# A two-layer Hyena and neighbourhood-attention step on one Trainium2 core: filter stage and input projection rewritten

## What is computed

```python
def hyena_filters(L, pe_w1, pe_b1, pe_w2, pe_b2, pe_w3, sin_freq, decay):
    ...
    hdn = jnp.sin(sin_freq[0] * (feats @ pe_w1 + pe_b1))
    hdn = jnp.sin(sin_freq[1] * (hdn @ pe_w2 + pe_b2))
    k = (hdn @ pe_w3).astype(jnp.float32) * (jnp.exp(-t * jnp.abs(decay)) + MOD_SHIFT)
    return k[:, :D_MODEL], k[:, D_MODEL:]          # k_fwd, k_bwd

def hyena_mixer(u, w_in, sconv_w, sconv_b, k_fwd, k_bwd, bias, w_out):
    z = centred_conv3(u @ w_in, sconv_w, sconv_b)
    x0, x1, v = jnp.split(z, 3, axis=-1)
    y = bidir_long_conv(v * x1, k_fwd, k_bwd, bias) * x0
    return y @ w_out
```

## Time and profile before

| | |
|---|---|
| median of 3 runs | 3693.0 us (3691.22 to 3696.77) |
| profiled execution | 3697.59 us, its span 3695.8 us |
| TensorE matmul busy | 3504.7 us, 95% of the span |
| VectorE / ScalarE / GpSimd busy | 1540.4 / 1036.7 / 1241.4 us |
| mean granted TensorE clock | 0.977 |

### The profile page before, as it was taken

The page is one execution under the profiler, slowest core; times in us unless marked ns, Lnnn a source line. Parts: engine busy times, 40 slices in busy tenths (PEclk is TensorE's granted clock), DMA queues, the critical chain, the costliest instruction groups (busy, mean ns, idle before and its releaser), DMA issues. The chain is left out here.

```text
span 3695.8 us, 47103 instructions
## 1 busy us (share of the span) xinstructions
PE 3504.7 (95%) x19104; PEld 3039.2 (82%) x19104; DVE 1540.4 (42%) x2528; ACT 1036.7 (28%) x1558; POOL 1241.4 (34%) x819
## 2 busy tenths in 40 slices
PE   7899998989999999999989998999989999999997
PEld 6888887778788888888878878888878888888886
DVE  7855544565344434444431015777340222111116
ACT  4421211233511111111342215777343111111113
POOL 5421114534422222222451304666352222222223
PEclk9899999999999999999999999999999999999998
DMA  3443325662122221221253446776201111111111
GB/s 133 129 170 109 108 81 175 215 229 74 52 75 74 77 72 63 69 69 63 80 180 126 163 164 171 177 177 155 92 23 41 40 40 35 40 40 35 41 41 63
DMA packets 173814, 365.92 MB, mean 99 GB/s; under 512 B 16967, under 2 KB 98439, under 8 KB 171944
## 3 DMA queue, kind: packets, MB, share of 16 engines
q1 hardware_dynamic: 168168, 352.55, 30.1%
q10 hardware_dynamic: 5440, 10.49, 0.9%
HBM read 285.38 MB, written 77.59 MB: 98 GB/s over the span
## 5 line engine op out<-in xcount | busy, mean ns | idle before, releaser
L150 POOL TENSOR_TENSOR w_lo<-w_raw,w_hi 128x1024 fp32r<-128x1024 f32 x207 | 502.8, 2429 | 1451.9 <-ACT w_hi L144 1451.8
L158 PE MATMUL ps_r<-a_hi,w_hi 128*128 128x512 f32 (+1 forms) x2496 | 889.8, 356 | 18.5 <-POOL a_lo L1933 10.6
L158 PE MATMUL ps_r<-a_lo,w_hi 128*128 128x512 f32 (+1 forms) x2496 | 885.7, 355 | 0.0
L158 PE MATMUL ps_r<-a_hi,w_lo 128*128 128x512 f32 (+1 forms) x2496 | 884.3, 354 | 0.0
L158 PEld LDWEIGHTS ps_r<-a_hi,w_hi 128*128 128x128 f32 x2496 | 473.5, 190 | 95.8 <-POOL a_lo L1933 18.6
L158 PEld LDWEIGHTS ps_r<-a_lo,w_hi 128*128 128x128 f32 x2496 | 473.7, 190 | 65.4 <-issue 1.2
L158 PEld LDWEIGHTS ps_r<-a_hi,w_lo 128*128 128x128 f32 x2496 | 473.1, 190 | 66.1
L144 ACT ACTIVATE w_hi<-w_raw 128x1024 fp32r<-128x1024 f32 x207 | 217.7, 1052 | 976.7 <-PE ps_r L158 555.5
L2132 DVE TENSOR_TENSOR hid_l<-hid_l,ps_r 128x1280 f32<-128x1280 f32 x44 | 65.5, 1488 | 824.3 <-PE ps_r L158 824.3
L2152 DVE SCALAR_TENSOR_TENSOR x_t_l<-ps_r,mod,x_t_l 128x1024 f32<-128x1024 f32 (+1 forms) x288 | 241.3, 880 | 260.3 <-PE ps_r L158 260.3
L158 PE MATMUL ps_in<-x_split_f,w_hi 128*128 128x512 f32 (+1 forms) x1152 | 312.6, 359 | 4.8 <-DVE gout_f L673 4.8
(11 more groups left out here) (259 smaller groups left out, 6015.8 us busy)
## 6 DMA issues: line engine op xcount, KB each, us to landing
w_raw<-in_w_all SPq DMA_DIRECT2D x213, 512.0 KB, 3.6
ada_w_l<-in_ada_t SPq DMA_DIRECT2D x59, 512.0 KB, 3.5
v_hl<-v_d SPq DMA_DIRECT2D x128, 128.0 KB, 2.9
t_tail_f<-in_ada_t SPq DMA_DIRECT2D x24, 512.0 KB, 4.1
spec<-gout_f SPq DMA_DIRECT2D x80, 128.0 KB, 2.3
g_spec_c<-spec ACTq DMA_DIRECT2D x20, 512.0 KB, 4.9
v_d<-z_v_l SPq DMA_DIRECT2D x10, 1024.0 KB, 4.5
q_hl_l<-q_d SPq DMA_DIRECT2D x32, 320.0 KB, 7.4
```

The lines of the kernel that those rows point to most:

```text
L150: pool.tensor_tensor(wl[:, s, 0:width], raw[:, s, 0:width], wh[:, s, 0:width].bitcast(F32), ALU.subtract).then_inc(w_split, 1)
L158: last = pe.matmul(out[:, c0:c1], w[:, c % 2, blk * 128:blk * 128 + 128], x[:, c0:c1], start=start and b == 0 and term == 0, stop=stop and ...
```

## The change

In the filter stage: the range reduction is three instructions instead of six (the factor 1/(2 pi) is multiplied into `fcol` once, the sine gets a scale); the backward kernel is multiplied in place in its PSUM bank, so that sum and difference read one operand from SBUF and one from PSUM; `taps` waits for `pq_ok` instead of `ker_ok`; basis entries have their own DRAM tensor and are loaded straight to the place of their low part, up to eight of them before the first step (entries 5 and 6 behind a wait for `pe_c`); two tiles are made at j = 0 and at j = 1 and one at j = 2 to 7; the row products run at j = 2 to 7 of q = 0 to 2; `gout` has three buffers; x is split one tile a step.

In the projection: entry 0 goes to the other `pg` tensor, so the wait for the last `combine` stands before entry 1; the eviction comes before the split of the later entry; the transposes of a block (i, cc) are made in role 0 of the next block, after its first and second column chunk (the last block keeps its own in role 2); the x0 result of the last block is evicted, convolved and stored in the forward stage, for which both stages share one PSUM allocation.

```diff
                 def phase(layer, h):
-                    dve.tensor_scalar(c, a, 1.0 / (2 * math.pi), MAGIC, ALU.mult, ALU.add).then_inc(dve_s, 1)
-                    dve.tensor_scalar(c, c, MAGIC, None, ALU.subtract).then_inc(dve_s, 1)
-                    dve.scalar_tensor_tensor(a, c, -TWO_PI_HI, a, ALU.mult, ALU.add).then_inc(dve_s, 1)
-                    dve.scalar_tensor_tensor(a, c, -TWO_PI_LO, a, ALU.mult, ALU.add).then_inc(dve_s, 1)
-                    dve.tensor_scalar(a, a, 3.1415925, -3.1415925, ALU.min, ALU.max).then_inc(arg_ok, 1)
+                    dve.tensor_scalar(c, a, MAGIC, None, ALU.add).then_inc(dve_s, 1)
+                    dve.scalar_tensor_tensor(a, c, MAGIC, a, ALU.subtract, ALU.subtract).then_inc(arg_ok, 1)
...
                 def generate(g):
-                    ker = win[:, g % 2, :, :].rearrange("p a b -> p (a b)")
+                    fwd, bwd, tap_b = win[:, g % 2, 0, :], win[:, g % 2, 1, :], gbank(g)[:, 256:512]
                     if g % 10 in (0, 8):
-                        dve.scalar_tensor_tensor(ker, ker, 0.05, gbank(g), ALU.add, ALU.mult).then_inc(zero, 1)
+                        dve.memset(win[0:1, g % 2, 1, :], -0.05).then_inc(zero, 1)
...
+                    dve.scalar_tensor_tensor(fwd, fwd, 0.05, gbank(g)[:, 0:256], ALU.add, ALU.mult)
+                    dve.scalar_tensor_tensor(tap_b, bwd, 0.05, tap_b, ALU.add, ALU.mult).then_inc(ker_ok, 1)
...
+                    dve.tensor_tensor(pq[:, g % 2, 0, :], fwd, tap_b, ALU.add)
+                    dve.tensor_tensor(pq[:, g % 2, 1, :], fwd, tap_b, ALU.subtract).then_inc(pq_ok, 1)
...
                 def taps(g):
-                        pe.wait_ge(ker_ok, g - 1)
+                        pe.wait_ge(pq_ok, g - 1)
...
+                def load_basis(j):
+                    sp.dma_start(basis_raw(j), t["filt"][j, :, 0:basis_width(j)]).then_inc(bs_in[j], 16)
...
-                return range(10 * q + 10 if j == 0 else 10 * q + j + 12, 10 * q + j + 13)
+                if j < 2:
+                    return range(10 * q + 10 + 2 * j, 10 * q + 12 + 2 * j)
+                return range(10 * q + j + 12, 10 * q + j + 13)
...
-            X_AFTER = {1: (0,), 2: (1,), 4: (2,), 5: (3,), 7: (4,), 9: (5, 6, 7)}
+            X_AFTER = {1: (0,), 2: (1,), 3: (2,), 4: (3,), 5: (4,), 6: (5,), 7: (6,), 9: (7,)}
...
                 # ScalarE, projection
-                            split_hi(act, ei + 2 + j, i, 6)
                             act.wait_ge(w_used, i * 6 + (ei + j + 1))
...
-                            act.activation(dst[:, :], pg[j % 2][:, 0:TOK], ACT.Identity,
+                            act.activation(dst[:, :], pin(j)[:, 0:TOK], ACT.Identity,
                                            scale=tile[:, 0, 1:2], bias=tile[:, 0, 3:4]).then_inc(z_ok, 1)
-                        high(i, cc, 2)
+                            split_hi(act, ei + 2 + j, i, 6)
...
                 # TensorE, projection
+                def turn(i, cc, n):
+                    if n == 1:
+                        pe.wait_ge(fold, i * 2 + (cc + 1))
+                        pe.wait_ge(tl_ok, 1 + i * 6 + 3 * cc)
+                        transposes(0)
+                        transposes(1)
+                    else:
+                        pe.wait_ge(tl_ok, 1 + i * 6 + (3 * cc + 1))
+                        transposes(2)
...
-                                for chunk in CHUNKS:
+                                for n, chunk in enumerate(CHUNKS):
+                                    if role == 0 and n:
+                                        turn(*before(i, cc), n)
...
             # forward stage
-            pf = [st.enter_context(nc.psum_tensor(f"ps_fw{g}", [128, 2048], F32)) for g in range(2)]
+            pf = [banks[:, 2048:4096], banks[:, 0:2048]]
+                    if f == 0:
+                        act.activation(gate[:, :], pf[1][:, 0:TOK], ACT.Identity, scale=conv_p[:, 23, 1:2],
+                                       bias=conv_p[:, 23, 3:4]).then_inc(z_ok, 1)
```

More of the change, by code:

```diff
@@ L207, in hyena_natten_step @@
             bas = [place(f"basis{b}", (X1, base_a + 40960)[b], [128, 5, 2, 1024], F32R) for b in range(2)]
+            bas_raw = [place(f"basis_raw{b}", (X1, base_a + 40960)[b], [128, 5, 2, 1024]) for b in range(2)]
             xs = [place(f"x_split{b}", (X0, X1)[b], [128, 4, 2, TOK], F32R) for b in range(2)]
@@ L224, in hyena_natten_step @@
             hs = place("hd_split", REST, [128, TOK], F32R)
-            gout = place("gout", REST + 5120, [128, 2, 2, 256])
+            gout = [[place(f"gout{b}{side}", (REST + 5120 + 2048 * b + 1024 * side, gaps[2 + side] + 2048)[b // 2], [128, 256])
+                     for side in range(2)] for b in range(3)]
             negt = place("negt", REST + 9216, [128, 10])
@@ L261, in hyena_natten_step, with before @@
             TR = ((0, 4, pt), (4, 8, pa), (8, 10, pt))
+            LAST = (3, 1)
+            def before(i, cc):
+                return (i, 0) if cc else (i - 1, 1)
             HALVES = ((0, 640), (640, TOK))
             ps_mlp = (pg[0], pta)
[L264 to L271, removed]
+            ROWS = {10 * q + j + 2: 6 * q + j for q in range(3) for j in range(2 * (16 - E_PE) // 3)}
+            LAST_ROW = max(ROWS)
             def bank(s):
@@ L581, in _ @@
                             j = 3 * cc + role
-                            if role == 2:
-                                high(i, cc, 0)
-                                high(i, cc, 1)
-                            split_hi(act, ei + 2 + j, i, 6)
+                            if role == 0 and i + cc:
+                                for r in range(3):
+                                    high(*before(i, cc), r)
+                            if role == 2 and (i, cc) == LAST:
+                                for r in range(3):
+                                    high(i, cc, r)
+                                split_hi(act, ei + 2 + j, i, 6)
+                                break
                             act.wait_ge(w_used, i * 6 + (ei + j + 1))
@@ L734, in _ @@
                             j = 3 * cc + role
-                            if role == 2:
-                                low(i, cc, 0)
-                                low(i, cc, 1)
-                            z, src = (za, zb, zb)[role], pg[j % 2]
+                            if role == 0 and i + cc:
+                                for r in range(3):
+                                    low(*before(i, cc), r)
+                            if role == 2 and (i, cc) == LAST:
+                                for r in range(3):
+                                    low(i, cc, r)
+                                break
+                            z, src = (za, zb, zb)[role], pin(j)
                             w = conv_p[:, i * 6 + j:i * 6 + j + 1, :]
@@ L1198, in _ @@
                             last.then_inc(c_mm, 1)
+        psum.close()
         e0 += E_INV
```

224 lines of the change are left out of this document (115 added, 109 removed).

## The result

The changed kernel takes 3631.42 us in the median of four runs (3629.33 to 3631.99), the kernel before 3693.78 us (3691.22 to 3696.77): a ratio of 0.983, 95% interval 0.9813 to 0.9847, 62 us faster. The forecast was 3620 with a range of 3606 to 3650: the direction and the range held, the middle was 11 us too low.

A forecast was written before the change was run, and what follows sets the result against it. TensorE, busy 95% of the span, was taken as the bound, so only its idle and slow time could be won. Gains of 47.8, 22.5 and 5.5 sum to 75.8 us; with 2 held back, about 3620 at the median, range 3606 to 3650.

The forecast's parts named there:

- Startup: Before the first transform: shorter range reductions and earlier tap tiles move its start from 63 to about 50.5, 12.5 us less.
- Transforms: Filter stage: waits for basis loads, w3 split and `generate` go; 117 us instead of 152.3, 35.3 us less.
- the floor: Transforms: TensorE's 936 matmuls at 0.12 us each, 112.3 us, the least the stage can take.
- 1 for steps 30 to 39: Last ten transform steps: 1 us allowed because x loads and stores share the queue.
- rival A: Filter stage stays paced by VectorE and GpSimd: 24 steps take 4.0 us instead of 3.36, 15 us, 3635; chance 0.22.
- forty more instructions: Transforms: splitting one 512-column VectorE instruction into two is free; by the skill's fixed cost it would be 6.3 us.
- Projection: Projection stage: seven blocks lose waits and half-rate matmuls, first entry follows busy TensorE; 22.5 us less.
- Cover of the fold: Projection: transposes come 19.6 us after role 1 instead of 12.3, covering about 8.4 us of eviction, convolution, product and fold.
- Between the stages: Gap between projection and forward matmuls: the last store moves to the next stage, 5.5 us less.
- B: Projection rival: a new wait at the transposes of seven blocks, 32 us less won, 3652; chance 0.10.
- C: Filter stage rival: `taps` waiting for `pq_ok` keeps TensorE at 1.2 GHz, 87 us, 3707, slower; chance 0.03.
- D: Rival of no effect: startup, steps and projection all fail, time stays within 0.2% (7.4 us); chance 0.03.

The follow-up runs named there:

- m_both: Changed kernel with row products moved to steps 6 to 9, 12 to 19, 22 to 27, and odd half copied before the weight split in steps 30, 31: 3633.87 us.
- u_sbuf: Changed kernel with the backward kernel's product put back into SBUF, sum and difference reading two SBUF operands, taps waiting for ker_ok: 3643.07 us.
- u_basis: Changed kernel with basis entries 4 to 9 loaded one by one behind stores and split two steps ahead of use, as before: 3633.93 us.
- u_gate: Changed kernel with the last block's x0 evicted, convolved and stored in the projection stage again: 3637.98 us.
- u_turn: Changed kernel with the projection's transposes back in role 2 of their own block, eviction still ahead of the weight split: 3629.47 us.
- run 19: Not a label: the words "in its profiled run 19 matmuls" mean 19 matmuls in the profiled run of u_turn.

## Why the prediction was right, and where it was not

*Startup, right.* First transform at 50.73, forecast about 50.5; taps(2) at 27.78, forecast 27.8. The last term fits better than its own working: GpSimd's queue was 21.1 us from 28.5 on, which is 49.6, and what makes it 50.7 are short gaps in that queue (0.80, 0.36 and 0.32 us in the trace) that the forecast doesn't name. The chain of causes held too: undoing the sine costs 4.4 us there and undoing the product 6.7, and the wait ahead of the first transform names GpSimd's `pq_low`.

*Transforms, the term that was mis-sized.* 117 us was forecast and 124.7 measured. By groups of ten steps the forecast's own terms give 31.6, 30.1, 30.1 and 25.5 (the floor of 29.3 or 24.5, the cold start, the turns, the last group's 1 us); measured were 35.3, 31.2, 30.0 and 28.2. The 3.7 us of the first group are the step "row product 1.29, combine 0.67, product 0.70, sum and difference 0.67 if unstretched": I took the stretch away from the sum and difference, and did not see that the row product has two operands in SBUF as well and was being moved from steps 9 to 26 into steps 2 to 7, beside the basis splits. m_both bears it out as far as it goes: with no row product in steps 2 to 5, and two fewer in the group, it takes 30.3 us. The combine rows of steps 2 to 7 are 3.87, 4.60, 4.21, 4.19, 3.65 and 3.27 us apart where 3.3 was written. In the second group, 1.1 over, TensorE waits 0.57 and 0.84 us at its two turns, for which 0.8 was allowed; the rest is not broken down. The 2.7 of the last group are the "1 for steps 30 to 39": that allowance was for queues, and the three TensorE waits there come from VectorE. Both are rival A, in four of the first and in some of the last steps and not in all: 7.7 us instead of its 15.

*What hid in the loads.* The forecast let the stage fall to TensorE's own work and so needed no share for each edit. By single undoing the transforms owe 7.9 us to the PSUM product and 5.5 to the early loads; the remaining 14 of 27.6 belong to no single edit tested (three `gout` buffers, `generate` placed two at a time, row products that no longer wait for `raw`, the earlier w3 split, the other `pg` tensor for entry 0) or to several together. Two waits of the earlier trace rows are nearly as much, 7.9 us for the w3 split and 4.8 ahead of the projection; both are gone in the changed kernel and in u_sbuf and u_basis too, so neither of these two edits is needed for that. Which edits are was not tested and stays open.

*VectorE beside GpSimd.* The 414 ns of L653 against the stretched L649 are what the Trainium skill (SBUF — State Buffer, "SBUF: two separate sides") says: a VectorE instruction with two SBUF inputs and a GpSimd instruction that reads SBUF hold a port pair in turn, each for its whole length. The trace agrees there and at the row product: that of 66.99 ends at 69.55, 1.09 us behind the end of the basis split, nearly a whole unstretched length. The forty more instructions were put at nothing and cost little: from L647 to L648 the starts are 0.33 us apart (61.66 to 61.99), as the earlier trace rows had it, but the sum that follows starts 0.79 us after the product in the median of the 40 tiles, where it was 0.71 before (in the 32 tiles without a zeroed row). That is 0.08 us a tile, some 3 us of VectorE in all, an estimate from these two medians; how much of it is on the path no run separates. It is about half of the 6.3 us that the prediction works out from the Trainium skill's 150 cycles. The instruction that writes PSUM takes 420 ns against 411.

*Projection, right sum, wrong cause.* 340.2 us was forecast and 340.1 measured. The step that failed is "Cover of the fold": it gave the gain to the late transposes, which the changed kernel can do without, and as the earlier trouble it cited the split of the earlier trace rows. That split, role 0's, waits 13.9 us in kernels with and without stalls. The harm came from the next one, and the line that moves the ada loads, which I had priced as "SP's ada loads pass one weight load; they are used 20 us later" and so as harmless, is by itself worth all of it. The eviction ahead of the split is worth it by itself too. Gains of edits that cure one wait don't add: in the kernel before each of the two alone takes the projection from 362.7 to 342 us, and all three with the earlier start to 340.1.

*Between the stages, right.* 4.88 us, forecast about 5; u_gate gives 5.8 back.

*The sum.* Forecast for the profiled execution 3623.6, measured 3629.33: 7.7 us of transforms, less the 2 held back. The rest of the 11.4 at the median is where a profiled run lies in its spread: the forecast took off 3.6 for the one before, which lay above its median, and the one after lies 2.1 below its own. Rivals: B did not occur (no wait for `low`), C did not (clock 1.00 in both stages), D did not.

## What to carry to other kernels

When two engines stretch each other, list every instruction of the pair that has the property, not the one with the largest row, and look at which of them the change moves beside the other; a steady duration before says nothing if its neighbours change. When a stall is followed back through a queue, go on to what each queue waits for, and check that the wait named is absent where the stall is absent: the 13.9 us split was the longest wait in sight and innocent. An in-order queue of loads should not have a load that waits for a slow consumer ahead of one that is due.

## What was not expected of the hardware

The scaling of x (L683) has one tensor input in SBUF and still took 3.16 to 3.33 us a pair beside a GpSimd split of 2.96, 1.12 alone. The sentence of the Trainium skill cited above also counts VectorE instructions in a two-port mode among those that hold the pair. No record names the mode, but the starts fit it. Alone, the 1024 columns of L683 hold VectorE for 0.72 us (165.62 to the second of the pair at 166.34) and its 256 columns for 0.32; the row product's 1024 columns hold it for 1.14 (80.38 to 81.52) and 256 columns of the other instructions for 0.33. So 768 more columns cost the scaling 0.40 us and the row product 0.81: it goes through long rows at twice the pace. All three stretches are in the part of 1024 columns (2.83, 3.01 and 2.99 us instead of 0.80); none is in the part of 256.

The same code can lose TensorE's clock in one run and keep it in another. u_turn's filter stage is the changed kernel's, its waits at the first turn were no longer (2.14 and 1.04 us against 2.15 and 1.52), and in its profiled run 19 matmuls behind the turn ran 0.21 us apart, at 1.2 GHz, in the changed kernel's none: the ten steps took 32.3 us against 31.2.

One line in the order of SP's loads was worth 18.7 us of 3694 (0.5%), more than the whole sine chain and the basis in place.
